# One inference step of a four-mixer decoder: all 1032 tokens together, against two token groups run one behind the other

## What is computed

```
u = rmsnorm(h) @ w_in                       # one projection, columns split among four head groups
A: causal conv (width 4), two block-diagonal gates, linear recurrence over time, times gelu(gate)
B: attention, window 128, 4 query heads, 2 key heads, rmsnorm and rotary on q and k, sinks
C: HGRN2, 4 heads of 64: state = decay * state + k v^T, decays per channel
D: mLSTM, 4 heads of 64: matrix memory with exponential input gate and a running maximum
h += concat(A, B, C, D) @ w_out
h += relu(rmsnorm(h) @ w_up)^2 @ w_down
h += sigmoid(h @ w_ple_gate) * (p[l] @ w_ple_proj)
```

## Time and profile before

| | |
|---|---|
| median of 3 runs | 3231.13 us (3225.46 to 3239.09) |
| the profiled execution's span | 3234.4 us |
| PE busy | 2971.1 us, 92% |
| DVE, ACT, POOL busy | 1149.4, 905.8, 905.2 us |

### The profile page before, as it was taken

One profiled execution on the slowest core, in us unless ns is written; L12 is line 12 of the kernel. 1 busy time (PEld: TensorE's weight loads), 2 busy tenths in 40 slices (PEclk: granted clock), 3 DMA queues, 4 the chain that ended last, 5 costly groups with the idle time before them and its releaser, 6 DMA issues.

```text
span 3234.4 us, 43899 instructions
## 1 busy us (share of the span) xinstructions
PE 2971.1 (92%) x18128; PEld 2801.4 (87%) x18128; DVE 1149.4 (36%) x2022; ACT 905.8 (28%) x1377; POOL 905.2 (28%) x591
## 2 busy tenths in 40 slices
PE   5988977889999999999968899778899999999999
PEld 4887865579999999999967788655899999999998
DVE  4643255553222222222355423566422222222223
ACT  4443222233111111113345332223331111111133
POOL 2111244222222332225131112432122223222251
PEclk8999976789999999999979999768899999999999
DMA  4010100021111111112210111000211111111112
GB/s 165 33 48 27 59 20 7 9 88 40 49 50 45 45 45 49 42 46 69 79 59 23 46 41 58 14 1 9 94 44 49 46 45 45 49 48 45 63 52 79
DMA packets 42756, 155.78 MB, mean 48 GB/s; under 512 B 6786, under 2 KB 8066, under 8 KB 41088
## 3 DMA queue, kind: packets, MB, share of 16 engines
q1 hardware_dynamic: 33696, 125.68, 11.3%
q10 hardware_dynamic: 8928, 28.28, 2.3%
HBM read 136.18 MB, written 17.76 MB: 48 GB/s over the span
## 4 chain that ended last, share of the span: by engine, by line
PE 81%; DVE 11%; ACT 3%; issue 3%; POOL 2%; DMA 0%; ACTq 0%; DVEq 0%; SPq 0%; POOLq 0%
PE pj L338 24%; PE pj L339 24%; PE pj L340 24%; DVE small L1648 2%; DVE ext L1334 2%; DVE ext L1843 1%; PE pm L351 1%; DVE small L1334 1%; PE pj L579 1%; DVE vt L1334 1%; PE pm L545 1%; PE pm L430 1%; POOL w_lo L1190 1%; PE pm L549 1%; PE pm L531 1%
## 5 line engine op out<-in xcount | busy, mean ns | idle before, releaser
L338 PE MATMUL pj<-m_hi,w_hi 128*128 128x344 f32 x1920 | 614.4, 320 | 0.0
L340 PE MATMUL pj<-m_hi,w_lo 128*128 128x344 f32 x1920 | 613.2, 319 | 0.0
L339 PE MATMUL pj<-m_lo,w_hi 128*128 128x344 f32 x1920 | 612.7, 319 | 0.0
L338 PE MATMUL pj<-n_hi,w_hi 128*128 128x344 f32 x1584 | 526.5, 332 | 71.9 <-DVE n_lo L1334 27.5
L340 PE MATMUL pj<-n_hi,w_lo 128*128 128x344 f32 x1584 | 516.1, 326 | 0.0
L339 PE MATMUL pj<-n_lo,w_hi 128*128 128x344 f32 x1584 | 516.0, 326 | 0.0
L339 PE MATMUL pj<-hid_lo,w_hi 128*128 128x344 f32 x1536 | 492.9, 321 | 0.0
L338 PE MATMUL pj<-hid_hi,w_hi 128*128 128x344 f32 x1536 | 490.8, 320 | 0.0
L340 PE MATMUL pj<-hid_hi,w_lo 128*128 128x344 f32 x1536 | 490.2, 319 | 0.0
L1243 POOL TENSOR_TENSOR w_lo<-w_raw,w_hi 128x1024 fp32r<-128x1024 f32 x128 | 308.4, 2409 | 628.6 <-ACT w_hi L1082 628.6
L1190 POOL TENSOR_TENSOR w_lo<-w_raw,w_hi 128x1024 fp32r<-128x1024 f32 x84 | 212.1, 2526 | 827.4 <-ACT w_hi L735 827.4
(11 more groups left out here) (330 smaller groups left out, 3430.5 us busy)
## 6 DMA issues: line engine op xcount, KB each, us to landing
w_raw<-in_w SPq DMA_DIRECT2D x216, 512.0 KB, 3.2
out_y<-res ACTq DMA_DIRECT2D x16, 516.0 KB, 2.7
res<-out_y ACTq DMA_DIRECT2D x2, 3096.0 KB, 11.2
res<-in_x SPq DMA_DIRECT2D x4, 1032.0 KB, 8.0
out_y<-res SPq DMA_DIRECT2D x8, 516.0 KB, 15.8
ext<-in_rope SPq DMA_DIRECT2D x2, 1032.0 KB, 12.5
res<-out_y ACTq DMA_DIRECT2D x2, 1032.0 KB, 4.9
hsq<-in_p ACTq DMA_DIRECT2D x2, 1032.0 KB, 4.7
```

The costliest lines, as they stand in the source:

```text
L338: pe.matmul(pj[:, t, 0:TT], wh, hi[:, k, cols], start=(k == 0), stop=False)
L339: pe.matmul(pj[:, t, 0:TT], wh, lo[:, k, cols], start=False, stop=False)
L340: last = pe.matmul(pj[:, t, 0:TT], wl, hi[:, k, cols], start=False, stop=(k == nk - 1))
```

## The change

The tokens are cut into two groups: A holds tokens 0 to 511, B holds tokens 512 to 1023 and the 8 sample tokens (520). The order of work is now: mixing of A in layer 1 (called q = 0); then for q = 0, 1, 2: `w_out` of group q, then the feed-forward of q with the mixing of the next one (q + 1) spread between its jobs, then the last gate of q; at the end the feed-forward and gate of q = 3. q = 0, 1, 2, 3 are A and B of layer 1, A and B of layer 2. `blend` gives each mixing step its share of dense jobs by count (1.02 jobs a step where B is mixed, 83 steps; 1.20 where A is mixed, 71 steps); each projection job of the mixing counts as one. Six feed-forward jobs are left for the end.

What follows from it in the code:
- Group A's dense column tile is 512 wide (one for each job), B's are 260 (two). Each weight block is loaded and split once for each group, 432 in place of 216. `w_raw` has 4 buffers, shared with `w_lo`, `w_hi` has 3.
- Three banks of `pj` are used in turn for each column tile (*shot*); PE waits for the eviction of the shot three before.
- The norm's factor is no longer multiplied into the activations. They are split as they are, and DVE multiplies the factor in when it evicts a projection. The norm's own matmul and the ACT instructions for its factor stand after the first projection job.
- DVE evicts the projection jobs; ACT did it before.
- Attention steps follow each other with one dense job between two; HGRN2 chunks are cut into three preparations (`hE`) and three products (`hP`), mLSTM chunks into two halves (`mc`), each with about one job between. For q = 0 there is no other group's dense work, so nothing stands between them.
- The whole program is unrolled, with no loop and no meeting of the engines between the layers.

```diff
-TT = T // 3
+HALF = SEQ // 2
+W = HALF + DEC
...
+RAW_BUFS, HI_BUFS, BANKS = 4, 3, 3
...
+TILES = (((0, HALF),), ((0, W // 2), (W // 2, W)))
...
+def feed(q):
+
+    o = []
+    for i in range(FF_STEPS):
+        for r in range(4):
+            o += [('up', q, i, r)] + ([('norm2', q)] if i == r == 0 else [])
+        o += [('down', q, i, d) for d in range(4)]
+    return o
...
+def blend(mix, ff, spare):
+
+    steps = sum(x[0] not in DENSE for x in mix)
+    dense = sum(x[0] in DENSE for x in mix) + len(ff) - spare
+    out, due, given, ff = [], 0.0, 0, list(ff)
+    for x in mix:
+        if x[0] in DENSE:
+            given += 1
+        else:
+            while given < due and ff:
+                out.append(ff.pop(0))
+                given += 1
+            due += dense / steps
+        out.append(x)
+    return out + ff
...
+    o = [('xin', 0, k) for k in range(KT)] + mixer(0) + [('ys', 0, k) for k in range(KT)]
+    for q in range(4):
+        for n in range(KT):
+            o += [('wout', q, n)] + ([('xin', 1, n)] if q == 0 else [])
+        o += blend(mixer(q + 1), feed(q), 6) if q < 3 else feed(q)
+        o += [('pload', q)]
+        for m in range(KT):
+            o += [('ple', q, m)] + ([('ys', q + 1, m)] if q < 3 else [])
+        o += [('pend', q)]
+    return o
...
+            def start_shot(s):
+                if s >= BANKS:
+                    pe.wait_ge(ev[s % BANKS], s // BANKS)
...
+            def factor(x):
+
+                q, acc, done = x[1], (nrm1 if x[0] == 'norm1' else nrm2), (nr1 if x[0] == 'norm1' else nr2)
+                for t, (c0, c1) in enumerate(TILES[q % 2]):
+                    s = SHOT[x] + t
+                    act.wait_ge(mm, s + 1)
+                    act.activation(acc[:, c0:c1], pj[:, s % BANKS, 0:c1 - c0], ACT.Ln, bias=EPS,
+                                   scale=1.0 / D).then_inc(ev[s % BANKS], 1)
+                    act.wait_ge(ev[s % BANKS], s // BANKS + 1)
+                    act.activation(acc[:, c0:c1], acc[:, c0:c1], ACT.Exp, scale=-0.5).then_inc(done, 1)
```

More of the change, by code:

```diff
@@ new lines, with _rank, _squares, _lanes @@
+W_ROW = _weight_rows()
+def _rank(kinds):
+    out, n = {}, 0
+    for x in ORDER:
+        if x[0] == 'job' and x[2] in kinds:
+            n += 1
+            out[x] = n
+    return out
+def _squares():
+    return {x: n + 1 for n, x in enumerate(x for x in ORDER if x[2:] and x[2] and (
+        x[0] in ('xin', 'wout') or x[0] == 'ple' and x[1] < 2))}
+def _lanes():
+    out, held = [], []
+    for x in ORDER:
+        if x[0] == 'ys':
+            out, held = out + held, []
+        if x[0] not in DENSE:
+            held.append((x, 0))
+            continue
+        halves = x[0] == 'ple' and x[1] % 2 or x[0] == 'down' and (x[3] or x[1] % 2)
+        parts = [(x, p) for p in range(2 if halves else 1)]
+        out += parts[:1] + held + parts[1:]
+        held = []
+    return out + held
@@ new lines, in whole, with job @@
+            def whole(x, hi, lo, first=None):
+                j = JOBS[x][0]
+                pe.wait_ge(lo_made, j + 1)
+                for t, cols in enumerate(TILES[x[1] % 2]):
+                    start_shot(SHOT[x] + t)
+                    products(SHOT[x] + t, cols, [(j, k) for k in range(KT)], range(KT), hi, lo, KT,
+                             first if t == 0 else None)
+            def job(x, _):
+                q, name = x[1], x[2]
+                whole(x, n_hi, n_lo, (lambda k: pe.wait_ge(nx_l, q * KT + k + 1)) if name == 'gates' else None)
@@ L419, in attn @@
+            def attn(x, _):
+                q, step = x[1:]
+                first = q % 2 == 0
                 c = step
@@ L726, in _ @@
+            steps = dict(job=job, norm1=norm, norm2=norm, wout=wout, up=up, down=down, ple=ple, rows=rows, gate=gate,
+                         rope=rope, rot=rotate, vt=vtrans, attn=attn, sattn=sattn, hdiag=hdiag, hsamp=hsamp, hP=hP,
+                         hnorm=gnorm, mnorm=gnorm, mprep=mprep, mc=mc, msamp=msamp)
+            pe.wait_ge(cst_ld, 32)
+            for x, part in LANES:
+                if x[0] in steps:
+                    steps[x[0]](x, part)
         @block.scalar
@@ L1329, in _ @@
+            split_lo(2)
+            for x in ORDER:
+                if x[0] in steps:
+                    steps[x[0]](x)
         @block.vector
@@ L1883, in _tiles @@
+            dve.memset(so[:], 0.0)
+            dve.wait_ge(cst_ld, 32)
+            for l in range(LAYERS):
+                lam(l)
+            for x in ORDER:
+                if x[0] in steps:
+                    steps[x[0]](x)
 def _tiles(w, k0, n):
```

2947 lines of the change are left out of this document (1510 added, 1437 removed).

## The result

The changed kernel takes **3363.0 us** (median, 3356.7 to 3366.3) against 3228.3 us for the kernel before in the same study: a ratio of **1.041, 95% interval 1.0385 to 1.0436**. It is 4.1% slower.

A forecast was written before the change was run, and what follows sets the result against it. PE, busy for 92% of 3234.4 us, bounds the kernel. Dense 2428 + mixing matmuls 356 + waits (38 + 135 + 176 + 48 + 15) = 3196 us; the 8-in-10 range takes in 3047 and reaches to 3310.

The forecast's parts named there:

- Dense work: Dense matmuls of both layers: columns and matmuls stay as many, so 2428 us again.
- a floor: Rival, dense matmuls: short ones stay at 157.6 ns because a weight load sets their time; 3553 us, chance 3%.
- Mixing's own matmuls: PE's own matmuls in the mixing: same columns, nearly the same count, not hidden by spreading; 356 us.
- The start: Kernel start: first job no longer waits for the norm and ends at 43 us, 38 of them lost (before 55).
- The factor: Norm in B's mixing: table loads and short functions for each column tile, PE needs that bank twice; 8.5 us.
- the 450 us of waits: Whole kernel before: waits and low clock cost 450 us, the only part that can be saved; 412 after the change.
- Weights twice ... at nothing: Second load and split of weights on ACT and POOL: off PE's path while one job's distance is kept; costs nothing.
- POOL slows DVE's chains: Rival, mixing: POOL's extra two-input SBUF operations lengthen DVE's, PE waits; 78 us, 3274 us in all, chance 0.3.
- the rest 33: A's mixing under B's feed-forward (q = 2): waits other than the gate rows' 15 come to 33 of 48 us.
- sample attention and sample state 7: B's mixing under A's feed-forward (q = 1 and 3): the sample tokens' attention and state lose 7 us uncovered.
- 13.1 us a chunk uncovered as before: A's HGRN2 at q = 0: 13.1 us a chunk minus 5.4 own, four times, plus the first's preparation; loss 35.
- Passages and end, 15: Last gate to `w_out` three times and the kernel's end: 15 us of waits (before 47).

The follow-up runs named there:

- experiments 2 and 3: POOL's subtraction for the weights' low part cut from 1024 columns to 32: first in the changed kernel, 3240.5 us, then in the kernel before, 3218.0 us.
- experiment 6: Changed kernel with DVE taking feed-forward results out of their banks before it waits for the mixing step's matmuls: 3342.5 us, ratio 1.0353.
- light_repaired: Changed kernel with value cache load in two transfers, early eviction for B's feed-forward, and POOL's low-part subtraction cut to 32 columns: 3172.3 us, ratio 0.9821.
- experiment 5: Changed kernel with the sample tokens' key cache load issued earlier, 3356.8 us; then also their value cache load in two transfers, 3331.8 us.
- four: Changed kernel with split value cache load, B's early eviction, POOL's low part in halves, early factor table load, A's uncovered HGRN2 products before next preparations: 3299.1 us.

## Why the prediction was wrong

The sum's terms against the trace. Measured waits are the length of a stretch, less the dense matmuls at 119.5 or 232 ns, less the mixing's own matmuls as the prediction's rates give them (82 us for A, 96 for B, which has the samples).

| part | forecast | measured |
|---|---|---|
| until the first matmul | 27 | 27 |
| rest of the start, A's mixing, q = 0 | 146 | 177 |
| B's mixing, q = 1 and 3 | 88, 88 | 93, 96 |
| A's mixing, q = 2 | 48 | 121 |
| `w_out`, gates, last feed-forward, end | 15 | 74 |
| **waits in all** | **412** | **588** |

**Right.** *Dense work* (2428 forecast, 2420 measured), and with it the 3% for a floor. *Mixing's own matmuls*: 356 forecast; the trace has 269 us at the high clock and 162 at the low one, 350 if the low one counts half. *The start*: the first job ends at 36.8 us (43 forecast). *The factor*: 6.3 us at the norm's second tile, for 8.5. *Places named ahead*: A's first gate matmul waits 12.3 us for DVE's convolution, and PE waits 9.5 us for the samples' mLSTM, for 10. *The saying that only the 450 us of waits could be saved.* (In telling where the 38 us come from, "a first layer that gains nothing" left out that by its own terms that layer's mixing goes from 174 to 223; the sum isn't touched.)

**Wrong: "Weights twice ... at nothing".** This is the step that failed. The second split costs 113 us more than before (experiments 2 and 3), not nothing. The term asked whether POOL and ACT keep one job's distance ahead of PE, and even that was off (28 us of waits for `w_lo`, 6 before). It didn't ask what POOL's instructions do to DVE. The rival "POOL slows DVE's chains" had the mechanism and a pair of rows for it, and priced it at 78 us with a chance of 0.3. Without the 22 us more for `w_lo` the 113 are some 90, so its size was near; with the other errors below, the measured 3363 us still lie far past its 3274. Its argument against, "HGRN2 and mLSTM keep slack of several us a job", doesn't hold: the slack exists on average, while a stretched operation of 2.9 us in front of an eviction is enough to stop PE. It should have been in the sum, since the change adds POOL work exactly beside DVE's mixing.

**Wrong: q = 2, "the rest 33".** It read the cover from jobs a step (1.20, more than B's 1.02). But here the cover is B's feed-forward with 260 columns, where a half job of `down` is a shot of 1.45 us and three banks hold 4.4 us. What counts is the time that the free banks hold, and what stands on DVE ahead of the next eviction; experiment 6 gives 32 us of it back, and in `light_repaired`, with POOL's part gone as well, this stretch is 64 us shorter, most of the 73 that it was over. "PE has three banks" stood in the prediction for the gate rows alone.

**Wrong: "sample attention and sample state 7".** One moved transfer was not followed: the value cache's load, hidden behind 100 us before, now stands 8 us ahead of its use, and takes 25. That is 31 us in both layers (experiment 5), and so the two 88s came out near the measured 93 and 96 by luck, by errors that cancel: in `light_repaired`, without POOL's part and this load, the two stretches are 50 and 48 us shorter, so that their waits are some 44 and 49, half of what the other terms had put there.

**Wrong: HGRN2 of A at "13.1 us a chunk uncovered as before"**. It is 19.3 us. PE in order of time, from one chunk's first matmul to the next one's:

```profile
240.63 3.74 PE L731 MATMUL pm<-sl 128*128 128x128 f32 x16 [2.97 <-DVE sl L1465]
248.39 1.19 PE L731 MATMUL pm<-sl,lev 128*128 128x128 f32 x4 [4.02 <-DVE att L1855]
...
252.97 0.79 PE L749 MATMUL pm<-qe,h_st 128*128 128x128 f32 x2 [0.87 <-DVE att L1855]
...
259.87 2.47 PE L731 MATMUL pm<-sl 128*128 128x128 f32 x10 [2.97 <-DVE sl L1465]
```

Four chunks make 25 us of the 31 us that this part is over. Three waits a chunk, of 7.9 us, stand where the earlier trace rows has two of 4.7. That is 3.2 of the 6.2 us; the rest is the clock. By stretch, the chunk of the earlier trace rows in the kernel before, then this one:

```profile
494.15:507.28 13.13, 7.85 (x52) 6.08 (x51) 9.53 (x27) 3.82 (x9) 7.29 (x16) 0.78 0.00 1
240.63:259.87 19.24, 11.38 (x51) 9.02 (x51) 12.04 (x36) 3.58 (x8) 7.16 (x17) 0.59 0.00 0
```

The same matmuls keep PE busy for 11.38 us in place of 7.85, at a granted clock of 0.59 in place of 0.78. One buffer for the prepared levels, so that a chunk's preparation follows the products of the last, would explain the third wait; only the order was varied (`four`), not the buffers, so it is argued, not shown.

**Wrong: "Passages and end, 15".** The factor of B's first norm is some 10 us of each stretch of A's `w_out`, which the prediction had booked with B's mixing; then come the gates of B (9 and 13 us, with `m_lo` late once and `w_lo` three times in each) and the last feed-forward (14, of which the norm's factor without cover is 8); some 18 us are short waits, not taken apart. The longest wait for `y_lo`, 10 us, stands ahead of the first `w_out` and so in A's mixing, where the forecast had 14 for norms and split of y.

**Against the kernel before** the trace gives, summed over all matmuls: PE's waits 237 to 358 us (+120), dense work 2466 to 2545 (+78), mixing 504 to 431 (-73), start and end +5; together the 130 us between the spans. So the mixing did become cheaper for PE, since fewer of its matmuls run at the low clock (960 before, 673 now). But now the clock falls in the dense work instead: 202 of its matmuls started at the low level before, 581 now, in stretches of 3 to 7 us that mostly follow or hold a wait of 2 to 6 us. That is 41 of the 78 us; the others are pauses too short to be listed as waits.

## What to carry to other kernels

Work that is added to POOL beside DVE's operations on SBUF is not free because POOL is idle: a DVE operation from SBUF that begins while POOL's runs is lengthened by up to 2.2 us here, most of POOL's 2.66, so the work has to be priced on DVE, at the places where PE waits for DVE. Cover is measured at the narrowest place, by the time that PE can work before it needs the next free bank, and by what stands in front of that eviction, not by an average of jobs a step. And when steps move, each transfer that they issue has to be followed: how long it takes, and how far ahead of its use it stands afterwards.

## What the hardware did that I had not expected

- A load of 127 partitions of 4 KB ran on one of 16 transfer engines, at 26 GB/s; as 112 and 15 partitions the same bytes landed in 5 us, before they were needed.
- POOL's subtractions for the weights (1042 us, 128 after the cut) cost DVE 232 us of busy time, with no change in DVE's work. Cut in four, they cost DVE 135 and POOL itself 232 more.
- A DVE operation from SBUF stands until POOL's is over only if it begins after it: with 512 columns, 15 that POOL joined late took 0.69 us, and 38 of 42 that began during a POOL operation ended 0.55 us after its end.
- Dense matmuls follow one line from 256 to 512 columns (118, 119, 157, 232 ns at 256, 260, 344, 512), so tile width costs nearly nothing by itself at these sizes. Yet 256 in place of 512 columns made this kernel 176 us slower, 123 of them in the two feed-forwards of A under a mixing, where the banks hold half the time.
